# A decoder step on one Trainium2 core: forty turns of the identity, x turned ahead of its sums, and two copies moved to GpSimd

## The reference

```python
def rms_norm(x, g):
    xf = x.astype(F32)
    y = xf * lax.rsqrt(jnp.mean(xf * xf, axis=-1, keepdims=True) + EPS)
    return (y * g.astype(F32)).astype(x.dtype)
...
    for layer in range(DEPTH):
        kind, idx = layer % N_MIXERS, layer // N_MIXERS
        g = P['norm_g'][layer]
        h = rms_norm(x, g[0])
        if kind == 0:
            y, c_new, h_new = rglru_mixer(h, ...)
...
        x = x + rms_norm(y, g[1])
        h = rms_norm(x, g[2])
        y = memory_cross_attn(h, mem_k[layer], mem_v[layer], P['x_w_q'][layer], P['x_w_o'][layer])
        x = x + rms_norm(y, g[3])
```

## Time and profile before

| | before |
|---|---|
| median of 3 runs | 2017.1 us (2013.8, 2017.1, 2017.39) |
| span of the profiled execution, first to last instruction | 2015.7 us; its own time is not listed beside it |
| instructions | 35615 |
| PE, PEld, DVE, ACT, POOL busy | 97%, 88%, 62%, 46%, 50% of the span |
| mean granted clock of TensorE | 0.986 of 2.4 GHz |
| chain that ended last | PE 75%, DVE 14%, ACT 5%, issue 2%, DMA 2% |

### The profile page before, as it was taken

The page is one execution under the profiler, slowest core; times in us unless marked ns, Lnnn a source line. Parts: engine busy times, 40 slices in busy tenths (PEclk is TensorE's granted clock), DMA queues, the critical chain, the costliest instruction groups (busy, mean ns, idle before and its releaser), DMA issues.

```text
span 2015.7 us, 35615 instructions
## 1 busy us (share of the span) xinstructions
PE 1951.5 (97%) x13890; PEld 1763.9 (88%) x13890; DVE 1244.4 (62%) x2220; ACT 930.6 (46%) x1557; POOL 1008.8 (50%) x1249
## 2 busy tenths in 40 slices
PE   7999999999999999999999999999999999999997
PEld 5998989798888988897889999999998889989976
DVE  5988342426887787755147777777454157874552
ACT  3676522334555555342354444443243347674333
POOL 4776704026555655250356666566631337776602
PEclk8999999999999999999999999999999999999998
DMA  4444476535444544487353444444586344445870
GB/s 130 149 147 135 135 250 231 208 105 174 124 116 132 151 132 140 138 297 241 113 170 108 130 130 130 137 136 146 165 313 211 132 148 141 135 148 166 292 231 27
DMA packets 332615, 324.64 MB, mean 161 GB/s; under 512 B 19768, under 2 KB 313056, under 8 KB 332448
## 3 DMA queue, kind: packets, MB, share of 16 engines
q1 hardware_dynamic: 330944, 321.49, 49.8%
q10 hardware_dynamic: 1504, 0.87, 0.2%
HBM read 292.16 MB, written 29.61 MB: 160 GB/s over the span
## 4 chain that ended last, share of the span: by engine, by line
PE 75%; DVE 14%; ACT 5%; issue 2%; DMA 2%; POOL 1%; SPq 1%; DVEq 0%; ACTq 0%
PE ps L773 10%; PE ps L774 10%; PE ps L778 10%; PE ps L1458 5%; PE ps L1467 4%; PE ps L1261 3%; PE ps L1524 2%; PE ps L888 2%; PE ps L763 2%; PE ps L765 2%; PE ps L764 2%; ACT wh L1713 2%; DVE work L2543 2%; PE ps L1602 1%; PE ps L1541 1%
## 5 line engine op out<-in xcount | busy, mean ns | idle before, releaser
L1693 POOL TENSOR_TENSOR wl<-raw,wh 128x256 fp32r<-128x256 f32 x1216 | 1003.3, 860 | 979.1 <-ACT wh L1713 978.9
L1713 ACT ACTIVATE wh<-raw 128x1024 fp32r<-128x1024 f32 x304 | 311.8, 1053 | 202.1 <-PE ps L778 49.8
L773 PE MATMUL ps<-Hh,wh 128*128 128x320 f32 x1200 | 372.2, 324 | 2.8 <-DVE work L2563 0.9
L774 PE MATMUL ps<-Hl,wh 128*128 128x320 f32 x1200 | 360.4, 314 | 0.0
L773 PEld LDWEIGHTS ps<-Hh,wh 128*128 128x128 f32 x1200 | 230.0, 192 | 11.3 <-DVE work L2427 2.3
L774 PEld LDWEIGHTS ps<-Hl,wh 128*128 128x128 f32 x1200 | 230.4, 192 | 2.1
L2258 DVE TENSOR_SCALAR work<-ps 128x512 f32<-128x512 f32 (+8 forms) x220 | 100.3, 474 | 170.9 <-PE ps L871 39.8
L778 PE MATMUL ps<-Hh,wl 128*128 128x320 f32 x1200 | 201.1, 310 | 0.0
L778 PEld LDWEIGHTS ps<-Hh,wl 128*128 128x128 f32 x1200 | 183.2, 189 | 0.1
L773 PE MATMUL ps<-Oh,wh 128*128 128x320 f32 x512 | 152.2, 310 | 3.7 <-DVE Ol L3004 3.7
L774 PE MATMUL ps<-Ol,wh 128*128 128x320 f32 x512 | 151.1, 308 | 0.0
(11 more groups left out here) (439 smaller groups left out, 3922.0 us busy)
## 6 DMA issues: line engine op xcount, KB each, us to landing
raw<-rg_w_in SPq DMA_DIRECT2D x128, 256.0 KB, 3.5
raw<-hg_w_in SPq DMA_DIRECT2D x128, 256.0 KB, 4.8
raw<-ssd_w_in SPq DMA_DIRECT2D x96, 256.0 KB, 3.9
work<-cache_mem_k SPq DMA_DIRECT2D x40, 512.0 KB, 6.3
work<-cache_mem_v SPq DMA_DIRECT2D x40, 512.0 KB, 5.1
raw<-rg_w_out SPq DMA_DIRECT2D x64, 256.0 KB, 3.6
raw<-x_w_k SPq DMA_DIRECT2D x64, 256.0 KB, 3.6
raw<-x_w_v SPq DMA_DIRECT2D x64, 256.0 KB, 3.7
```

The source lines that it names most:

```text
L773: pe.matmul(ps[:, bank, 0:n], high(half, k), mh[:, k, 0:n], start=(k == 0), stop=False)
L774: pe.matmul(ps[:, bank, 0:n], high(half, k), ml[:, k, 0:n], start=False, stop=False)
L1693: ins = pool.tensor_tensor(out, src, wh[:, parted(n) % HALVES, r:r + 2].bitcast(F32), ALU.subtract)
L1713: act.activation(wh[:, nx.n % HALVES], raw[:, slot, :, half * P:(half + 1) * P], ACT.Copy).then_inc(hi_ready, 1)
```

## The change

It makes four edits. TensorE turns the identity forty times into 128 columns of bank 7 after `consts` and before it waits for x. All eight tiles of x are turned first; sums 0 to 3 follow, then the parameter turns, then sums 4 to 7. GpSimd copies the high parts of units 0 and 1 as soon as block 0 has landed, ahead of its subtractions. ScalarE starts its count of splits at 2, and waits for those two copies before it splits unit 2.

```diff
@@ TensorE
             pe.wait_ge(*past("consts", 1))
+            for n in range(40):
+                pe.transpose(ps[:, 7, 0:P], ident[:], ident[:])
             pe.wait_ge(*past("in_x", 32))
             for k in range(KD):
...
                 mm.then_inc(S("pro_full"), 1)
-                if k >= 2:
-                    sum_square(0, 3, k - 2)
+            for k in range(4):
+                sum_square(0, 3, k)
             pe.wait_ge(*past("in_par", 16 * 12))
...
-            sum_square(0, 3, 6)
-            sum_square(0, 3, 7)
+            for k in range(4, KD):
+                sum_square(0, 3, k)
             pe.wait_ge(*past("in_mem", 32))
@@ GpSimd
+            for n in range(2):
+                pool.wait_ge(landed[0], 64)
+                pool.tensor_copy(wh[:, n], raw[:, 0, :, n * P:(n + 1) * P]).then_inc(hi_ready, 1)
             for n in PARTED:
                 low(n)
@@ ScalarE
-            nx = Count()
+            nx = Count(2)
...
                 n = PARTED[nx.n]
+                if nx.n == 2:
+                    act.wait_ge(hi_ready, 2)
```

## The result

The changed kernel takes 1998.5 us in the median of six runs (1995.0 to 2003.4); the kernel before, run beside it, takes 2017.2 (2011.9 to 2020.1). The ratio is 0.9915, 95% interval 0.9895 to 0.9935. The profiled execution took 2002.3 us, its span is 2000.5, 15.2 under that of before.

A forecast was written before the change was run, and what follows sets the result against it. TensorE, busy 1951.5 of 2015.7 us, bounds the kernel, then the start's chain of waits without slack. Gains 5.2 + 4.8 + 0.8 = 10.8 take the span to 2004.9, the median to 2006.3; range 2001.5 to 2014.5.

The forecast's parts named there:

- so the transfers move with the work: After the start: weights are requested when earlier ones are used up, so the start's cost is hardly made up later.
- The stream's end: Forty turns before x: start at about 1.85, end at 8.3 us (bounds 7.9 and 10.45); clock rise given 8 in 10.
- The tiles of x: Eight tiles turned ahead at 0.42 each, 8.3 to 11.7 us; with sums, VectorE starts at 18.8, not 24.04: gain 5.2.
- GpSimd's copies: High parts of units 0 and 1: 1.2 us per copy, ready at 13.2; the eight subtractions then end at 19.1.
- dear copies: Rival: GpSimd's copies take 3.0 us each, Hl ends 2.5 later; 2008.8 us; chance 0.12.
- VectorE from the root to the last Hl: Normalisation to last low part: 9.4 us instead of 14.2, with L2291 undisturbed by GpSimd; gain 4.8.
- The clock behind it: Denser Hh products: gain 1.6 us if TensorE's level holds, 0 if it falls once more; 0.8 taken.
- The early sum: First 60 us: gains of 5.2, 4.8 and 0.8 sum to 10.8 us.
- no rise: Rival: clock does not rise while TensorE turns; VectorE starts at 27.1, 3.1 later; 2014.6 us; chance 0.15.
- no overlap: Rival: each turn waits for the last, 0.42 us each, stream ends at 18.7; 2022.8 us; chance 0.05.
- Absorption: Rival: a later transfer that does not move with the work absorbs the gain; about 2015 to 2017; chance 0.06.

The follow-up runs named there:

- small_40: Kernel before plus only 40 turns of 32x32 ahead of the wait for x: 2010.2 us, ratio 0.9969.
- the one with sixteen: Changed kernel with 16 full turns instead of 40: 2010.7 us, ratio 0.9960.
- mix_72: Changed kernel with 30 full turns and 42 of 32x32 in place of the 40 full ones: 2006.3 us, ratio 0.9942.
- 72, 128: Kernel before plus 72 or 128 turns of 32x32 ahead of the wait for x: 2016.0 us (0.9992) and 2019.0 us (1.0006).
- forty added in the second half: Kernel before plus 40 turns of 32x32 in first_two, at the head of the HGRN stage, about 1029 us: 2012.0 us, ratio 0.9972.
- 168 turns: Changed kernel with 168 full turns instead of 40: 2017.0 us, ratio 1.0001.

## Why the prediction was wrong, and where it was right

**The step that failed** is one that the prediction took in a single clause, "so the transfers move with the work", and used for the sum: that from the end of the start on the kernel is the old one, moved. The forty turns were costed by their time alone. As eighty instructions on TensorE's queue they bring some 7 us in the later stages: 7.3 by small_40, without any time of the start moved. The profile had the refills (the same line stands on the page of before) and I did not ask what moving them does. The one rival about the later stages had the gain absorbed; none had it grow.

Point by point:

- The stream's end: 8.3 forecast, 7.88 measured. It started at 1.79, the level rose 3.1 us later (4.3 taken, 3.5 was the near bound), and turns stand 0.109 apart, 0.213 at the low level. That this execution came out better than forecast is luck: over the profiles the rise took 2.8 to 6.0 us. The "does turning raise the clock" question is answered: yes, in every profile with full turns, the one with sixteen included. The Trainium skill's rule ("TensorE: Matmul & The Clock Gate", Part 4) that turning does not count as TensorE's activity for the clock disagrees with this trace, where the level rose 3.1 us into turning and nothing else; the measurement decides.
- The tiles of x: 0.57 each, not 0.42. The rows I used were shares of the chain of waits, for a tile turned alone at the end of the old order. The timeline of before, shown above, has that tile and the sum behind it 0.52 apart from start to start, and eight in a row take 0.57 (128 columns of x take 0.18, those of the identity 0.109); I have no row that says why x is slower. It costs 1.2 us. The sums gave 0.7 of that back, since four in a row take 2.26 and not 2.6, and the stream's end 0.3: VectorE starts at 19.23, against 18.8. **Gain 4.8 for 5.2,** with misses of opposite sign in it.
- GpSimd's copies: 2.02 for two, so 1.0 each, for 1.2 taken between 1.05 and 3.0, and about what ScalarE takes for the same tile (1.05). The Trainium skill ("GPSIMD Engine Reference", section 4.1) has one-input operations there at roughly line rate, and the trace agrees. Low parts over at 19.05 for 19.1. (In the rival of dear copies, 16.8 and eight subtractions at 0.743 give 22.7, not 23.7; nothing hangs on it.)
- VectorE from the root to the last Hl: 9.41 for 9.4. **Gain 4.8 for 4.8.** The SSD stage of the old trace was the right row, since it was the same sequence with the same neighbour idle.
- The clock behind it: the low level came once more, at 28.82, for 3.4 us instead of 10.2. Against 0.8 forecast, what is left of the 10.0 after 4.8 and 4.8 is 0.4. With the copies alone the level did not fall at all and 1.7 was left: so both cases of the forecast occur.
- The early sum was thus 10.0 for 10.8. Right in mechanism and size.
- From span to runs I took 1.4; the profiled executions stand 1.7 to 1.9 over their spans.
- The range: its lower end had 4.8 us under the forecast for the stream, the clock and the spread. A term for how much later stages move when their instructions do was missing. By small_40 against before it is 7 us.

The rivals: dear copies, no rise and no overlap are each excluded by one row above. Absorption is excluded for the turns; of the copies' early gain, some 2 are missing at the end both alone (6.5) and with the order (5.9), for which I have no cause.

What stays open: why the number of instructions matters. Shown is that it does with times unchanged (small_40 against before, mix_72 against the changed kernel), that the number matters and not the presence (72, 128), and that forty added in the second half are enough for most of it. Not shown: that it goes by 256 (168 turns speak against a pure rule), that the delayed weights are the path, or that it is the place of the boundaries at all. A longer list also changes the size of the program and so where program and data may lie in memory; no run here keeps the size and moves the boundaries of the second half.

## What to carry to other kernels

Cover a known wait at the start with work of TensorE that needs nothing, and let it last to the end of the wait; move GpSimd's two-input work off VectorE's critical stretch. Both did here what rows of the old trace said, to half a microsecond in sum. But when a long unrolled kernel changes by more than its edited part explains, add the same number of idle instructions to the old one before crediting the idea: 7 of this change's 17 us are such an effect, may be gone with the next edit on that queue (72 turns of either size and 128 small ones have little or none of it), and a scan of the number is a cheap last step of tuning (of the numbers tried here forty is the best, and no version beat the changed kernel).

## What the runs showed of the hardware that was not expected

- Forty pairs of tiny instructions in a wait make a 2017 us kernel 7.3 us faster with every early time unchanged (ratio 0.9969, 0.9953 to 0.9984); with 72 (0.9992) and 128 (1.0006) the interval takes in no change.
- A refill of TensorE's instruction queue (16 KB, 256 instructions) in flight goes with a weight transfer that lands 0.3 to 0.4 us later.
- A stream of turns alone raised the level from 1.2 to 2.4 GHz, 2.8 to 6.0 us after its start in the eleven profiles that have one. Behind sixteen of them it rose at 4.58 and fell at 8.00 after 2.9 us of idling, and stayed low for another 10.2 us of gapless turning and summing.
- Turning x runs at 0.18 us for 128 columns where turning the identity runs at 0.109, both at the high level.
